# Settling of the two longest tiles' limits moved into the attention, one mask step per pair, query stores issued by ScalarE

## What is computed

```python
def block(i):                                   # 128 queries, tile i of 8
    sc = indexer_scores(qib, wib, ki, valid)    # (128, keys)
    _, sel = lax.top_k(sc, 256)                 # tiles 0 and 1: all valid keys
    return sparse_attend(qb, take_rows(k, sel), take_rows(v, sel), ...)
# sparse_attend: q is rotated (partial_rope), s = q k / 8, softmax over the selected, times v
```

## Time and profile before

| | us |
|---|---|
| median of 3 runs | 2648.32 |
| lowest to highest | 2641.32 to 2650.43 |
| profiled execution | 2653.54 |
| its span in the profile | 2651.7 |
| TensorE, matmuls busy | 2492.7 (94%) |
| VectorE busy | 1803.1 (68%) |
| ScalarE busy | 1115.7 (42%) |
| GpSimd busy | 1290.1 (49%) |

### The profile page before, as it was taken

The page is one execution under the profiler, slowest core; times in us unless marked ns, Lnnn a source line. Parts: engine busy times, 40 slices in busy tenths (PEclk is TensorE's granted clock), DMA queues, the critical chain, the costliest instruction groups (busy, mean ns, idle before and its releaser), DMA issues.

```text
span 2651.7 us, 51288 instructions
## 1 busy us (share of the span) xinstructions
PE 2492.7 (94%) x19930; PEld 2299.6 (87%) x19930; DVE 1803.1 (68%) x3096; ACT 1115.7 (42%) x2040; POOL 1290.1 (49%) x974
## 2 busy tenths in 40 slices
PE   6879979999998999999999989999889999999999
PEld 4748854667798999999999989999889999999999
DVE  6588978665248756656667687767695756656775
ACT  5155646775136444444212363332454444442223
POOL 2403642343125656566544535545345656555454
PEclk7999979999899999999999999999999999999999
DMA  9305657202333444344894333328324434359831
GB/s 320 95 20 154 207 200 242 65 2 78 114 103 113 134 135 155 123 154 141 333 341 165 114 97 106 106 84 325 97 87 156 145 123 163 122 196 365 295 137 70
DMA packets 319028, 409.87 MB, mean 155 GB/s; under 512 B 42192, under 2 KB 229672, under 8 KB 315978
## 3 DMA queue, kind: packets, MB, share of 16 engines
q1 hardware_dynamic: 316010, 404.68, 45.7%
q10 hardware_dynamic: 2784, 1.97, 0.3%
HBM read 284.78 MB, written 119.85 MB: 153 GB/s over the span
## 4 chain that ended last, share of the span: by engine, by line
PE 60%; DVE 17%; issue 7%; DMA 6%; POOL 5%; ACT 3%; ACTq 1%; SPq 1%; DVEq 0%; POOLq 0%
PE PS L2445 9%; PE PS L2447 9%; PE PS L2446 9%; PE PS L2489 5%; PE PS L2491 5%; PE PS L2492 5%; PE PS L588 3%; PE PS L1824 3%; PE PS L1853 2%; PE PS L1835 2%; POOL ring L2764 2%; DMA t_scratch<-stage 1%; DVE s_all L1522 1%; POOL stage L2777 1%; DVE th L3018 1%
## 5 line engine op out<-in xcount | busy, mean ns | idle before, releaser
L2445 PE MATMUL PS<-th,ring 128*128 128x264 f32 x2800 | 802.8, 287 | 28.0 <-DVE y L2968 9.3
L2447 PE MATMUL PS<-th,ring 128*128 128x264 f32 x2800 | 799.1, 285 | 0.0
L2446 PE MATMUL PS<-th,ring 128*128 128x264 f32 x2800 | 798.2, 285 | 0.0
L2445 PEld LDWEIGHTS PS<-th,ring 128*128 128x128 f32 x2800 | 530.2, 189 | 35.2 <-issue 31.4
L2446 PEld LDWEIGHTS PS<-th,ring 128*128 128x128 f32 x2800 | 530.3, 189 | 0.0
L2447 PEld LDWEIGHTS PS<-th,ring 128*128 128x128 f32 x2800 | 530.2, 189 | 0.0
L2764 POOL TENSOR_TENSOR ring<-wraw,ring 128x512 fp32r<-128x512 f32 x232 | 340.5, 1473 | 360.2 <-ACT ring L2568 359.7
L2764 POOL TENSOR_TENSOR ring<-sums,ring 128x512 fp32r<-128x512 f32 x216 | 320.0, 1483 | 278.1 <-ACT ring L2568 277.9
L2489 PE MATMUL PS<-th,ring 128*128 128x264 f32 x1232 | 353.8, 287 | 14.6 <-DVE zs L3078 6.3
L2491 PE MATMUL PS<-th,ring 128*128 128x264 f32 x1232 | 352.3, 286 | 0.0
L2492 PE MATMUL PS<-th,ring 128*128 128x264 f32 x1232 | 351.9, 286 | 0.0
(11 more groups left out here) (368 smaller groups left out, 5155.0 us busy)
## 6 DMA issues: line engine op xcount, KB each, us to landing
t_scratch<-stage SPq DMA_DIRECT2D x154, 528.0 KB, 3.4
th<-t_scratch SPq DMA_DIRECT2D x77, 1056.0 KB, 8.8
wraw<-in_ffn_w_gu_dram SPq DMA_DIRECT2D x96, 512.0 KB, 5.3
wraw<-in_ada_w_dram SPq DMA_DIRECT2D x80, 512.0 KB, 4.8
wraw<-in_ffn_w_down_dram SPq DMA_DIRECT2D x80, 256.0 KB, 6.1
wraw<-in_conv_w_in_dram SPq DMA_DIRECT2D x28, 512.0 KB, 5.1
y<-y_scratch SPq DMA_DIRECT2D x12, 1056.0 KB, 9.8
y_scratch<-y SPq DMA_DIRECT2D x6, 2112.0 KB, 8.4
```

The lines of the kernel that those rows point to most:

```text
L2445: pe.matmul(out, hi, x[:, TH, k, :], start=(k == 0 and i in (1, 2, 5)), stop=False, skip_group_check=True)
L2446: pe.matmul(out, hi, x[:, TL, k, :], start=False, stop=False, skip_group_check=True)
L2447: last = pe.matmul(out, lo, x[:, TH, k, :], start=False, stop=(k == 3), skip_group_check=True)
```

## The change

Three things. `dve_select` no longer settles the limits of entries 0 and 1; it copies their `kk` to SBUF. A new `dve_settle_step` does it in four steps for each, in front of that tile's six mask steps. `dve_masks_at` takes one step per pair from a list of 50, pairs 0 to 49, instead of 1.5 of 42 in pairs 0 to 27. The steps' scratch `mscr` moves to two of the four slots of the split weights, and ScalarE waits for all masks before it writes the last of these slots, at pair 55. SyncE's `store_q` goes; ScalarE issues each query store after the swap of the chunk two later.

```diff
@@ -443,6 +443,7 @@
             ("psgB", [P, 2, CH], F32), ("pafB", [P, 2, CH], F32), ("qcB", [P, 2, CH], F32), ("ktok", [P, 4, 256], F32),
             ("junkB", [P, 384], BF16))
         (_c, junkC) = layout(("_c", [P, A0 + 4416], F32), ("junkC", [P, LS], BF16))
+        (mscr,) = place(AREA["ring"] + 2 * KT * P, ("mscr2", [P, 2, SEQ], F32))
         qst = qst_[:]
         ada_stage = qstage[:].rearrange("p (a x) t -> p a (x t)", a=4)[:, 2:4, :]
         cm = qstage[:].rearrange("p k t -> p (k t)")
@@ -781,10 +782,12 @@
             sp.dma_start(ki_prompt.rearrange("o b (t p) d -> p (o b t) d", p=P), kiw[:, 0:8, 0:64]).then_inc(ki_stored, 16)
             sp.dma_start(ki_sample.rearrange("o b t d -> (o b t) d"), kiw[0:NS, 8, 0:64]).then_inc(ki_stored, 16)
 
-        def store_q(sp, t, chunks=range(NCH)):
-            for n in chunks:
-                sp.wait_ge(fin_rdy, R_AT[9 + t] + n + 1)
-                sp.dma_start(q_scr[:, t, chunk(n)], qst[:, n, :]).then_inc(q_stored[n], 16)
+        def act_store_q(act, r):
+
+            if R_AT[9] <= r < R_AT[16]:
+                t, n = divmod(r - R_AT[9], NCH)
+                act.wait_ge(fin_rdy, r + 1)
+                act.dma_start(q_scr[:, t, chunk(n)], qst[:, n, :]).then_inc(q_stored[n], 16)
 
         def sp_proj_b(sp):
             for p in STEPS:
@@ -798,8 +801,6 @@
                             v_sample.rearrange("o b t g d -> (o b t) (g d)")
                         sp.wait_ge(evac, M_AT[6] + tt + 1)
                         sp.dma_start(vo, v_tok[0:w, tt, :]).then_inc(out_stored if tt < 8 else vs_stored, 16)
-                if p > 9:
-                    store_q(sp, p - 10)
                 if 11 <= p <= 13:
                     for tt in range(3 * (p - 11), 3 * (p - 11) + 3):
                         w = P if tt < 8 else NS
@@ -1029,6 +1030,7 @@
                     act_evac_rope(act, p, n, psgB)
                     act_count(act, 2 * (ITEM_AT[p] + n))
                     act_swap(act, R_AT[p] + n)
+                    act_store_q(act, R_AT[p] + n - 2)
                     if n == 0:
                         for q in NEXT_W[6 if p == 8 else 8]:
                             proj_hi(act, q)
@@ -1639,17 +1642,30 @@
             tiny = 1.1754943508222875e-38
             link(dve, dve.scalar_tensor_tensor(out=v(th, 0, NA), in0=v(th, 0, NA), scalar=tiny, in1=v(th, 0, NA),
                                                op0=ALU.is_ge, op1=ALU.mult))
-            for j in range(NA):
-                s, rows, L, k = entries[j]
-                A = relu[:, j, 0:L]
-                link(dve, dve.tensor_scalar(A, s, one(th, j), -NEG, ALU.is_le, ALU.mult))
+            link(dve, dve.tensor_copy(bv[:, BS + E * kk:BS + E * kk + NA], v(kk, 0, NA)))
+            link(dve, dve.tensor_tensor(v(cand), v(th), v(sig), ALU.mult))
+
+        def dve_settle_step(dve, entries, j, step):
+
+            s, rows, L, k = entries[j]
+            A, B = mscr[0:rows, 0, 0:L], mscr[0:rows, 1, 0:L]
+            cnt, ge, kk, sig, th, cand, inc = (bv[0:rows, BS + 7 * x + j:BS + 7 * x + j + 1] for x in range(7))
+            if step == 0:
+                link(dve, dve.tensor_scalar(A, s, th, -NEG, ALU.is_le, ALU.mult))
+            elif step == 1:
                 link(dve, dve.tensor_tensor(A, A, s, ALU.max))
-                link(dve, dve.tensor_reduce(one(cand, j), A, AX_X, ALU.min))
-                link(dve, dve.tensor_scalar(A, s, one(cand, j), 0.0, ALU.is_ge, ALU.add, accum_out=one(cnt, j)))
-            link(dve, dve.tensor_tensor(v(ge, 0, NA), v(cnt, 0, NA), v(kk, 0, NA), ALU.is_ge))
-            link(dve, dve.tensor_tensor(v(inc, 0, NA), v(ge, 0, NA), v(cand, 0, NA), ALU.mult))
-            link(dve, dve.tensor_tensor(v(th, 0, NA), v(th, 0, NA), v(inc, 0, NA), ALU.max))
-            link(dve, dve.tensor_tensor(v(cand), v(th), v(sig), ALU.mult))
+            elif step == 2:
+                link(dve, dve.tensor_reduce(cand, A, AX_X, ALU.min))
+            else:
+                link(dve, dve.tensor_scalar(B, s, cand, 0.0, ALU.is_ge, ALU.add, accum_out=cnt))
+                link(dve, dve.tensor_tensor(ge, cnt, kk, ALU.is_ge))
+                link(dve, dve.tensor_tensor(inc, ge, cand, ALU.mult))
+                link(dve, dve.tensor_tensor(th, th, inc, ALU.max))
+                link(dve, dve.tensor_tensor(cand, th, sig, ALU.mult))
+
+        def mask_steps(j):
+
+            return [(j, step) for step in range(-4 if j < NA else 0, 6)]
 
         def dve_mask_step(dve, entries, j, step):
 
@@ -1682,8 +1698,13 @@
 
         def dve_masks_at(dve, entries, n):
 
-            for x in range(3 * n // 2, 3 * (n + 1) // 2 if n < 28 else 0):
-                dve_mask_step(dve, entries, (2, 5, 4, 3, 1, 0, 6)[x // 6], x % 6)
+            steps = [x for j in (2, 5, 4, 3, 1, 0, 6) for x in mask_steps(j)]
+            if n < len(steps):
+                j, step = steps[n]
+                if step < 0:
+                    dve_settle_step(dve, entries, j, step + 4)
+                else:
+                    dve_mask_step(dve, entries, j, step)
 
 
         def smp_turn_k(pe, b, a):
@@ -1978,6 +1999,8 @@
                     if n and g == 0:
                         act_out(act, n - 1)
                 act_pair_chunks(act, n)
+                if n == 55:
+                    act.wait_ge(mask_rdy, 7)
                 if n in (49, 52, 55, 58):
                     split_hi(act, "out", (n - 49) // 3, MM0["out"])
             act_out(act, NPAIR - 1)
```

## The result

| | before | after |
|---|---|---|
| median | 2646.63 (2641.32 to 2650.43, 4 runs) | 2670.53 (2667.81 to 2672.50, 4 runs) |
| profiled execution | 2653.54 | 2667.81 |
| its span | 2651.7 | 2666.0 |

The ratio is 1.0091 with a 95% interval of 1.0069 to 1.0113: the change costs 24 us (18 to 30). The forecast was 2665.7, in a range of 2646 to 2676, slower with a chance of 0.72. Sign and range held. Of the three terms the largest was 1.3 us off, the other two 2 us each.

A forecast was written before the change was run, and what follows sets the result against it. The prediction took a chain of waits, 60% held by matmuls, as the bound. Its terms 4 - 2 + 15.4 = +17.4 us on a median of 2648.3 gave 2665.7 us, range 2646 to 2676.

The forecast's parts named there:

- The settling is not on the path: Before the attention: removing some 9.9 us of VectorE settling gains nothing, as the third pair's scores wait for ScalarE's swap chain.
- by-product: GpSimd's rotation beside the settling, 1.90 us against 0.93 elsewhere, speeds up; up to 1.5 us, unused because ScalarE is later.
- The gate: Third pair's scores, waiting for the last rotated query, come 4 us later with stores on ScalarE; bounds -2 and +6.
- The lag of the search: VectorE's search before the attention: 3.8 us late from stores in steps 10 to 12, plus 1.26 near the end.
- two more stores between the last evacuations, 1.26: End of ScalarE's query work: two stores delay the last swap by 1.26 us, or 0.64 at the cheaper store price.
- the last landing: The last swap's transfer after its issue, beside SyncE's query loads: 2.0 to 4.9 us, taken near the contended end.
- Pairs 0 to 27: Early attention: one mask step per pair instead of one and a half saves 2 us; bounds -4 and 0.
- Pairs 28 to 49: Steps ahead of the copy out of the single bank make TensorE wait, from pair 32 on: +15.4 us, bounds 0 and 22.
- The rival that the steps hide: From pair 32 on, early copies or the three pairs of lookahead absorb the steps: 2650 us, chance 0.18.
- The hole closes and the clock stays: Before the attention: TensorE's 7.4 us idle goes, half speed shrinks by about 8 us: 2637 us, chance 0.09.
- ScalarE's lateness reaches TensorE: Late evacuations or adaLN chunks: gate +8 instead of +4, 2 to 4 us more in pairs 0 to 10; 2673, chance 0.08.
- Signs: Expected in the trace: TensorE idle 10 to 17 us at second-half transposes, third score at 387 to 390, ScalarE stores of 0.6 us.

The follow-up runs named there:

- e4: The kernel before without the settling passes of tiles 7 and 6, nothing in their place: 2645.58 us, ratio 1.0009.
- e2: The kernel before with only the query stores moved to ScalarE, settling and masks as before: 2651.77 us, ratio 1.0011.
- e3: The whole change, but each pair's mask step stands behind both copies of the second half instead of ahead of the first: 2655.99 us, ratio 1.0027.
- e7: The whole change with the stores back on SyncE and each mask step behind the copies of the second half: 2650.46 us, ratio 1.0017.
- e1: The whole change with the query stores back on SyncE, masks and settling as changed: 2665.42 us, ratio 1.0049.
- e5: The kernel before, with SyncE issuing the last adaLN chunks of steps 14 to 16 ahead of its store waits: 2645.69 us, ratio 1.0002.
- e6: The whole change with all 50 steps done in pairs 0 to 31, before the second halves begin: 2659.65 us, ratio 1.0062.
- e11: The whole change with SyncE's second and third query load held back until the last rotated query is made: 2678.11 us, ratio 1.0114.

## Why the prediction was right, and where not

**The settling is not on the path.** Right. Without it, in e4, the gate is 0.9 us earlier, no more than the spread of such kernels, and the total +2 us (-2 to 7). The reasoning, that the later of two waits is the one to price, held. So did its by-product: tile 7's comparison pass took 1.83 us in the gap and, moved into the attention,

```profile
513.75 1.22 DVE L1656 TENSOR_TENSOR mscr<-mscr,s_all 128x1024 f32<-128x1024 f32 x1
```

and GpSimd's rotation, 1.90 beside it, is 0.93 without it. GpSimd's instruction before the rotation, of the kernel before:

```profile
370.54 1.42 POOL L1087 TENSOR_TENSOR qcB<-psgB,ropeC 128x352 f32<-128x352 f32 x1 [0.41 <-ACT psgB L994]
```

The Trainium skill (SBUF — State Buffer, "SBUF: two separate sides") says that whichever starts first has the shared port for its whole instruction and the other waits. The trace agrees, with each waiting in turn: VectorE's pass began at 371.21 while the row above ran (to 371.96) and is 0.61 us longer, and the rotation began at 371.92 while that pass ran (to 373.04) and is 0.97 longer.

**The gate, +4 taken, +6.0 measured.** The lag of the search was predicted at 3.8 plus 1.26; it was 4.1 plus 1.0. That agreement is partly luck: a store costs 0.45 us of issue, not the 0.63 of the same queue's swaps, and ScalarE had less slack than I credited. (By the prediction's own terms 0.45 would give 3 x 1.0 less 0.8, some 2.2 us, where 4.1 were measured.) The term "two more stores between the last evacuations, 1.26" named the wrong link: there the chain goes through the rotation of r = 42, whose swap now landed beside the first query load (3.66 us). From the evacuation of chunk 42 to the last swap that adds 0.66, and the swap began at 380.70 where the prediction had it ready at 380.0: 0.7 of the miss of 2. The rest is the last landing: 5.14, outside the bounds of 2.0 to 4.9 and 1.4 above the 3.8 that +4 implies. I had split the difference with "near the contended end"; with two query loads and four adaLN chunks in flight the contended row was the one to take. The bound of +6 was just met. (At the other end, stores of 0.32, the prediction's terms add up to -1.7 to +1.2, not -1.6 to +1.4; nothing rests on it.) What this gate is worth in the median is less sure than the gate itself: e2 says 3 (-1 to 7), e3 against e7 3, the whole change against e1 5 to 11.

**Pairs 0 to 27, -2 taken, 0 measured.** This step failed. After minus before is -2.8 in stage B, and on one pair of profiles it would pass for a hit. The table says otherwise: with the clock back after 6 to 7 us, B is 107.4 and 107.7 at one and a half steps (e2, e4) and 107.9 and 107.6 at one (e3, e7). In those two the step stands elsewhere; with it in the changed kernel's place, e1 has 111.9 at 18 us of half clock, against 111.9 and 111.2 at 19 in before and e5. The 0.92 us of idle in 450 to 460 that I doubled is gone after, yet other idle took its place. The difference between the two profiles is the clock: half speed lasted 19 us past the third scores in one and 10 in the other. Between 7 and 19 us of it lie some 4 us of B in kernels that are alike there.

**Pairs 28 to 49, +15.4 taken, +16.7 measured** (172.0 less 155.3; 15.9 in e1). Right in size, place and cause. Of the 16.7, 0.8 is the clock's dip at 533 us, which the prediction didn't have; e1, without it, has 15.9. By pairs, from the waits of e1's weight loads: 2.19 us at the scan (2.09 predicted), 1.95 in pair 38 (1.87), 1.67 in pair 37 (1.62). Two pairs are off by more: 32 with 0.99 (0.70), and 35 with 0.84 (1.37), because I priced the comparison pass at its 1.83 beside GpSimd and it took 1.22 here. Those two partly cancel in the sum. e3 moves the same steps behind the copy and 13.3 of the 16.7 go; e6 takes them out of these pairs and all goes. The rival that the steps hide fell with it: VectorE's idle third is there, and it covers all but 3.4 of some 22 us of steps when they stand where the slack is.

**The sum.** 6.0 + 0 + 16.7 = 22.7, inside both measured intervals (18 to 30, 13 to 23); predicted 17.4. The misses, of 2, 2 and 1.3 us, went the same way.

**The other rivals.** "The hole closes and the clock stays": the hole is closed in after and in e5, the clock fell to half in both, and e5 is worth 0 (-4 to 5). (The prediction had the clock fall after the idle 7.4 us; windows of 2 us put the fall at 369.7, within the idle that began at 367.3, and in the changed kernel at 376.0, within the pause that began at 371.2.) TensorE's pause only moved, 12.71 us at one wait; the clock's return at 388 to 416 us is not tied to the hole. "ScalarE's lateness reaches TensorE": its +8 on the gate didn't come, though +6 lies between it and the forecast, and TensorE's waits for adaLN chunks in 400 to 500 us are 2.5 us against 1.6.

**Signs.** TensorE idle at the transposes 11.1 us (10 to 17 named), TensorE at 7 to 9 tenths in 510 to 550, counts 5 us late, SyncE's stands at stores gone: all seen. The third score at 390.5 was just outside 387 to 390, the stores at 0.45 below 0.6.

## What to carry to other kernels

Before clearing an engine's work out of a gap, find which of the waits at the gap's end is the last; the work here was hidden, and its removal gained nothing that the total shows. Spare time of an engine has a place: put the filler behind the step that releases the bottleneck's single buffer, not ahead of it; that choice alone was 13 of 17 us here. And compare stages that repeat (here to 0.5 us between executions of one program) before spans that don't (4 to 10 us), or a returning clock passes for a gain.

## What the runs showed of the hardware

- The time at which TensorE's granted clock returned to 2.4 GHz after the same pause varied between executions of one program: 403.6 and 394 us in the kernel before, 400 and 416 in the changed one; some 4 us of the kernel's time hang on it. The Trainium skill (TensorE: Matmul & The Clock Gate, "Part 1") says that the warm-up varies from run to run and is worth under 1% of a typical kernel; these rows agree with both, 4 us of 2650 being 0.15%.
- Issue time on ScalarE's queue depends on the DMA: 0.45 us for the store of 128 rows to memory, 0.63 for a swap of 8 rows within SBUF. The store took SyncE 0.32.
- A small swap was used 1.4 us after its issue when the DMA engines fell idle (e11), 3.7 beside the first query load (after), and 4.9 (before) and 5.1 (after) with query loads and adaLN chunks in flight.
- VectorE's and GpSimd's instructions that collided waited for each other in turn: 1.83 us for a pass of 1.22, 1.42 and 1.90 for two of 0.93.
- A wait at a transpose shows in two rows. The stage's growth is that of the weight loads' row (16.2 against 15.9 us in e1, 3.5 against 3.4 in e3), not that of the matmuls' (11.7 and 2.0).
